# Two-head attention units with one-pass transposes, and modulation products on the matrix engine

## The reference, cut to what matters

```python
def first_block(x, c, ctx, c_ctx, w_ada, b_ada, ...):
    xc = ctx
    s_lat = jax.nn.silu(c)
    s_ctx = jax.nn.silu(c_ctx)
    for l in range(DEPTH):                                   # DEPTH = 2
        mod = (s_lat @ w_ada[l] + b_ada[l])[:, None, :]      # 1024 -> 6 * 1024
        sh1, sc1, g1, sh2, sc2, g2 = jnp.split(mod, 6, axis=-1)
        mod_c = s_ctx @ w_ada[l] + b_ada[l]
        ...
        h = modulate(rmsnorm(x, norm1_g[l]), sh1, sc1)
        hc = modulate(rmsnorm(xc, norm1_g[l]), csh1, csc1)
        p = h @ w_in[l]                # glu 1024, q k v 3 * 512, gates 2048
        ...
        y_conv = conv_branch(...)      # 31 taps over 512 channels, layernorm
        y_attn = merge_heads(neighbourhood_attention(q, k, v, k_c, v_c, na_rpb[l])) @ w_na_out[l]
        x = x + g1 * gated_merge(p[..., QKV_END:], y_conv, y_attn, w_out[l])
        x = x + g2 * conv_ffn(modulate(rmsnorm(x, norm2_g[l]), sh2, sc2), ...)
        if not last:                   # the same for the context, context_attention
            ...                        # over its own 256 keys
```

## Time and profile before

| | us |
|---|---|
| median of 3 runs | 2594.62 |
| lowest and highest | 2591.86, 2596.06 |
| the profiled execution | 2591.45 |
| its span in the profile | 2589.8 |
| mean granted clock of PE, of its full speed | 0.955 |

### The profile page before, as it was taken

The page is one execution under the profiler, slowest core; times in us unless marked ns, Lnnn a source line. Parts: engine busy times, 40 slices in busy tenths (PEclk is TensorE's granted clock), DMA queues, the critical chain, the costliest instruction groups (busy, mean ns, idle before and its releaser), DMA issues.

```text
span 2589.8 us, 49983 instructions
## 1 busy us (share of the span) xinstructions
PE 2318.4 (90%) x18080; PEld 2250.5 (87%) x18080; DVE 1991.8 (77%) x3466; ACT 1254.1 (48%) x1965; POOL 119.9 (5%) x231
## 2 busy tenths in 40 slices
PE   3778699977978999989999999998899999986998
PEld 3767599966878999977999999996899999976998
DVE  7998887969967876896899577668776677687555
ACT  3335266333455654435565454445544544565543
POOL 0000000000000000000000000001000000000000
PEclk9889799988989999989999999998999999998999
DMA  6544555764456555432587667674587587563654
GB/s 252 195 138 153 189 172 180 245 219 133 152 176 203 179 172 185 165 122 90 196 272 262 186 234 261 202 244 156 187 283 242 174 280 252 166 209 95 199 169 135
DMA packets 148461, 500.19 MB, mean 193 GB/s; under 512 B 16480, under 2 KB 17504, under 8 KB 147040
## 3 DMA queue, kind: packets, MB, share of 16 engines
q1 hardware_dynamic: 113472, 375.06, 42.8%
q0 software_dynamic: 32544, 119.03, 15.3%
q10 hardware_dynamic: 2304, 4.20, 0.6%
HBM read 497.16 MB, written 1.05 MB: 192 GB/s over the span
## 4 chain that ended last, share of the span: by engine, by line
PE 67%; DVE 19%; DMA 5%; ACT 4%; issue 4%; DVEq 0%; SPq 0%; POOL 0%; POOLq 0%; ACTq 0%
PE bank_pair L1415 20%; PE bank_pair L1417 20%; PE bank_pair L1416 20%; DVE w_lo L852 4%; DMA modraw<-in_w_mod 4%; DVE arena L1018 3%; DVE modraw L865 2%; DVE x_res L865 2%; PE bank_pair L1590 1%; PE ps_o L1628 1%; PE ps_t L1422 1%; PE ps_t L1601 1%; DVE arena L977 1%; ACT w_hi L494 1%; DVE h_lo L983 1%
## 5 line engine op out<-in xcount | busy, mean ns | idle before, releaser
L852 DVE TENSOR_TENSOR w_lo<-raw,w_hi 128x1024 fp32r<-128x1024 f32 (+3 forms) x772 | 839.9, 1109 | 290.2 <-ACT w_hi L494 287.9
L1415 PE MATMUL bank_pair<-h_hi,w_hi 128*128 128x256 f32 x3344 | 959.6, 287 | 24.6 <-DVE w_lo L852 24.6
L1416 PE MATMUL bank_pair<-h_lo,w_hi 128*128 128x256 f32 x3344 | 952.6, 285 | 0.0
L1417 PE MATMUL bank_pair<-h_hi,w_lo 128*128 128x256 f32 x3344 | 952.3, 285 | 0.0
L494 ACT ACTIVATE w_hi<-raw 128x1024 fp32r<-128x1024 f32 (+3 forms) x772 | 734.3, 964 | 432.9 <-PE bank_pair L1417 327.9
L1415 PEld LDWEIGHTS bank_pair<-h_hi,w_hi 128*128 128x128 f32 x3344 | 648.4, 194 | 36.2 <-DVE w_lo L852 22.5
L1416 PEld LDWEIGHTS bank_pair<-h_lo,w_hi 128*128 128x128 f32 x3344 | 648.7, 194 | 0.2
L1417 PEld LDWEIGHTS bank_pair<-h_hi,w_lo 128*128 128x128 f32 x3344 | 648.3, 194 | 0.0
L1415 PE MATMUL bank_pair<-e_both,w_hi 128*128 128x256 f32 x1774 | 514.7, 290 | 86.5 <-DVE e_both L1369 28.9
L1416 PE MATMUL bank_pair<-e_both,w_hi 128*128 128x256 f32 x1774 | 510.4, 288 | 0.0
L1417 PE MATMUL bank_pair<-e_both,w_lo 128*128 128x256 f32 x1774 | 509.8, 287 | 0.0
(11 more groups left out here) (208 smaller groups left out, 2252.2 us busy)
## 6 DMA issues: line engine op xcount, KB each, us to landing
modraw<-in_w_mod POOLq DMA_DIRECT2D x224, 512.0 KB, 4.6
raw<-in_w_gu SPq DMA_DIRECT2D x176, 512.0 KB, 4.8
raw<-in_w_up SPq DMA_DIRECT2D x132, 512.0 KB, 4.7
raw<-in_w_gate SPq DMA_DIRECT2D x48, 512.0 KB, 4.6
raw<-in_w_dn SPq DMA_DIRECT2D x64, 384.0 KB, 3.6
raw<-in_w_dn SPq DMA_DIRECT2D x64, 320.0 KB, 2.9
raw<-in_w_down SPq DMA_DIRECT2D x48, 384.0 KB, 3.8
raw<-in_w_down SPq DMA_DIRECT2D x48, 320.0 KB, 3.1
```

The costliest lines, as they stand in the source:

```text
L852: nc.vector.tensor_tensor(w_lo[:, p, at], raw[:, p, HALF * f:HALF * f + w], w_hi[:, p, at].bitcast(F32), ALU.subtract).then_inc(lo_ready, 1)
L1415: nc.tensor.matmul(out, l[0], r[0], start=start, stop=False)
L1416: nc.tensor.matmul(out, l[0], r[1], start=False, stop=False)
L1417: return nc.tensor.matmul(out, l[1], r[0], start=False, stop=stop)
```

## The change

There are two parts. **Modulation:** the 33 first blocks leave DVE. The host packs them transposed, so that a 128x128 piece can be PE's weights, and both vectors lie as the two columns of `ccol` (from the new input `vector_cols`). `pe_mod` makes 16 fp32 products of 2 columns for a block into `ps_mod`, four columns of `ps_t`, and ACT copies them to `modcol` (`mod_copy`), which frees `ps_mod`. PE does a block before its slab. At the start PE does blocks 0 and 1, then the sum of the squares, then 2 to 7. In the context branch the blocks are placed anew: one with every slab of glu, q and k, half a block with one of v, none in the gate stage. The load of x no longer waits for the last block and is issued by POOL behind block 8, and SP issues the first slab's first half ahead of blocks 6 and 7. Blocks from 33 on stay on DVE.

**Attention:** a unit is two heads and one tile of queries. The gate slab of unit h goes with it, not one unit later; its sums use all of the first pair of banks (`ps_gate`), the scores the second (`ps_s`). ACT scales the probabilities, so that the transposes are one-pass (`nc.tensor.transpose`) against the plain identity; ACT also copies the context's scores for x. In the context's own attention the maximum and the exponential read PSUM directly. Scores and values take the two heads in turn, on 64 partitions each.

The core of the diff, added lines above all (what they replace is in the functions printed above), with the indentation cut:

```diff
+CONV_AT = np.cumsum([0] + [CONV_SLAB] * 6 + [8] + [3, 8] * 4 + [8]).tolist() + [CONV_K * CONV_C]
...
         early = l == 0 and x == "ctx"
+        stage("glu", a[f"w_glu{l}"], SLAB, 2, mods=1 + early)
+        stage(qk, a[f"w_q{l}"], SLAB, 1, mods=2 if early else int(l == 0), arg=dict(dst="q", rope=rope, scale=HD ** -0.5, conv=(l, 0, 2)))
+        stage(qk, a[f"w_k{l}"], SLAB, 1, mods=2 * early, arg=dict(dst="k" if rope else "kc", rope=rope, scale=1.0, conv=(l, 2, 4)))
         stage("v", a[f"w_v{l}"], SLAB, 1, mods=int(early), arg=dict(dst="v" if rope else "vc", conv=(l, 4, 6), heads=NA_H))
+        stage("gate", a[f"w_gate{l}"], SLAB, 4, mods=int(l == 0 and not early), arg=dict(l=l, ctx=x == "ctx"))
...
+        ps_mod = ps_t[:, 1, 0:4]
+        ps_gate, ps_s = pb
...
+    load(first, 0, 0)
     for k in (6, 7):
+    sp.wait_ge(mod_mm, 2 * (k - 5))
...
+    def mod_copy(m):
+    act.wait_ge(mod_mm, 2 * m + 2)
+    nc.scalar.activation(modcol[:, :, bass.ds(2 * m, 2)], ps_mod.rearrange("p (c v) -> p v c", c=2), ACT.Copy)\
+        .then_inc(mod_done, 2)
+    def mod_copies(s, b, p):
+    if s.m0 < N_DOUBLE:
+        if s.mods == 2:
+            mod_copy(s.m0 + 2 * b + p)
+        if s.mods == 1 and p == 1:
+            mod_copy(s.m0 + b)
...
+    if i == 0:
+        for m in range(2, N_FIRST):
+            if m == 6:
+                split_hi((first, 0, 0), 0)
+                split_hi((first, 0, 0), 1)
+            mod_copy(m)
...
+            if h >= 1:
+                gate_copy(h - 1)
+            at = (h // 2, h % 2, h // 2 == s.bodies - 1)
+            split_hi(following(s, *at), 1)
+            if not is_ctx:
+                act.wait_ge(att_sum, NA_H * n["n_bias"] + h + 1)
+                wait_up(act, att_t, a0 + h - 1)
+                nc.scalar.activation(att_p[:, h % 2, :, 256:512], ps_s[:, :, 256:512], ACT.Copy)\
+                    .then_inc(att_cc, 1)
             act.wait_ge(att_max, a0 + h + 1)
+            if is_ctx:
+                wait_up(act, att_t, a0 + h - 1)
             for t in range(2):
+                scores = ps_s[:, t, 0:keys] if is_ctx else att_p[:, h % 2, t, :]
+                ins = nc.scalar.activation(att_p[:, h % 2, t, 0:keys], scores, ACT.Exp,
                                            bias=small[:, 4 + h % 2, t:t + 1],
                                            accum_out=small[:, 6 + h % 2, t:t + 1])
             ins.then_inc(att_exp, 1)
+            split_hi(after_next(s, *at), 0)
+            act.wait_ge(att_inv, a0 + h + 1)
+            for t in range(2):
+                ins = nc.scalar.activation(att_p[:, h % 2, t, 0:keys], att_p[:, h % 2, t, 0:keys], ACT.Copy,
+                                           scale=small[:, 6 + h % 2, 2 + t:3 + t])
+            ins.then_inc(att_norm, 1)
+        if h == NA_H:
+            gate_copy(h - 1)
...
             act.wait_ge(att_t, a0 + k + 1)
             wait_up(act, att_o, a0 + k - 1)
             nc.scalar.activation(
                 att_pt[:, k % 2, 0:nk, :].rearrange("p k (t q) -> p t k q", t=2),
                 ps_t[:, :, 0:keys].rearrange("p t (k q) -> p t k q", q=P), ACT.Copy).then_inc(att_tc, 1)
         if h >= 2:
+            c, t = (h - 2) // 2, (h - 2) % 2
+            act.wait_ge(att_o, a0 + h - 1)
+            nc.scalar.activation(e_hi[:, CONV_C + c, P * t:P * (t + 1)], ps_o[:, t, 0:P],
                                  ACT.Copy).then_inc(att_hi, 1)
...
             dve.wait_ge(att_s, a0 + h + 1)
+            if is_ctx:
+                scores = ps_s[:, :, 0:keys]
+            else:
+                wait_up(dve, att_t, a0 + h - 1)
+                dve.wait_ge(bias_in[h % 2], 16 * (NA_H // 2 * n_["n_bias"] + h // 2 + 1))
+                nc.vector.tensor_tensor(att_p[:, h % 2, :, 0:256], ps_s[:, :, 0:256], bias[:, h % 2, :, :],
+                                        ALU.add).then_inc(att_sum, 1)
+                scores = att_p[:, h % 2, :, :]
+            if 1 <= h < LN_AT:
+                conv_piece(l, 2 * h + 5, i)
+            if not is_ctx:
+                dve.wait_ge(att_sum, NA_H * n_["n_bias"] + h + 1)
+                dve.wait_ge(att_cc, NA_H * n_["n_bias"] + h + 1)
+            link(nc.vector.tensor_reduce(small[:, 4 + h % 2, 2:4], scores, AXX, ALU.max))
             nc.vector.tensor_scalar(small[:, 4 + h % 2, 0:2], small[:, 4 + h % 2, 2:4], -1.0, None,
                                     ALU.mult).then_inc(att_max, 1)
         if h < LN_AT:
+            conv_piece(l, 2 * h + 6, i)
         if h < NA_H:
+            at = (h // 2, h % 2, h // 2 == s.bodies - 1)
+            split_lo(following(s, *at), 1)
             dve.wait_ge(att_exp, a0 + h + 1)
+            nc.vector.reciprocal(small[:, 6 + h % 2, 2:4], small[:, 6 + h % 2, 0:2]).then_inc(att_inv, 1)
+            split_lo(after_next(s, *at), 0)
         if h >= 2:
...
+            c, t = (h - 2) // 2, (h - 2) % 2
+            at = slice(P * t, P * (t + 1))
+            dve.wait_ge(att_hi, a0 + h - 1)
+            nc.vector.tensor_tensor(e_lo[:, CONV_C + c, at], ps_o[:, t, 0:P],
+                                    e_hi[:, CONV_C + c, at].bitcast(F32), ALU.subtract).then_inc(att_lo, 1)
...
+        if h < NA_H:
+            mods(s, h // 2, h % 2)
...
+    def pe_mod(m, tile, halves=(0, 1), arrived=None):
+    for c in halves:
+        if arrived is not None:
+            pe.wait_ge(mod_in[c], arrived)
+        if c == 0:
+            wait_up(pe, mod_done, 2 * m)
+        for k in range(DC):
+            ins = nc.tensor.matmul(ps_mod[:, 2 * c:2 * c + 2], tile[:, c, P * k:P * (k + 1)], ccol[:, k, :],
+                                   start=k == 0, stop=k == DC - 1)
+        ins.then_inc(mod_mm, 1)
+    def mods(s, b, p):
+    if s.m0 < N_DOUBLE:
+        if s.mods == 2:
+            m = s.m0 + 2 * b + p
+            pe_mod(m, modraw, (0, 1), 16 * (m - N_FIRST + 1))
+        if s.mods == 1:
+            m = s.m0 + b
+            pe_mod(m, modraw, (p,), 16 * (m - N_FIRST + 1))
+    def first_mods(ms):
+    for m in ms:
+        pe.wait_ge(first_in[m], 16)
+        pe_mod(m, mod_first[m % 6])
...
     def body(b, is_first, last):
         for p in range(2):
+            mods(s, b, p)
             operands_ready(s, b, p, is_first)
...
+        first_mods(range(0, 2))
...
     ins.then_inc(sum_ready, 1)
+    if n["i"] == 0:
+        first_mods(range(2, N_FIRST))
...
         if h < NA_H:
+            wait_up(pe, att_exp if is_ctx else att_max, a0 + h)
+            c, t = h // 2, h % 2
+            for n_k, name in enumerate(("kc",) if is_ctx else ("k", "kc")):
+                for hd in range(2):
+                    r = HD * hd
+                    ins = nc.tensor.matmul(ps_s[:, hd, T * n_k:T * (n_k + 1)],
+                                           dst["q"][r:r + HD, c, t * P:(t + 1) * P],
+                                           dst[name][r:r + HD, c, :], start=True, stop=True)
             ins.then_inc(att_s, 1)
+            if h >= 2:
+                free_banks(s, h // 2, h % 2, False)
+            half(s, h // 2, h % 2, 0, h < 2)
+        if 1 <= h <= NA_H:
+            k = h - 1
+            pe.wait_ge(att_norm, a0 + k + 1)
+            wait_up(pe, att_tc, a0 + k)
+            for hd in range(2):
                 for q in range(nk):
+                    ins = nc.tensor.transpose(ps_t[:, hd, q * P:(q + 1) * P],
+                                              att_p[:, k % 2, hd, q * P:(q + 1) * P], table("ident"))
             ins.then_inc(att_t, 1)
         if h == LN_AT:
                 ins = nc.tensor.matmul(ps_o[:, 1, T:2 * T], ones, ln_y[:, k, :], start=k == 0,
                                        stop=k == CONV_C - 1)
             ins.then_inc(ln_var, 1)
+        if h < NA_H:
+            half(s, h // 2, h % 2, 1, h < 2)
         if h >= 2:
+            c, t = (h - 2) // 2, (h - 2) % 2
+            pe.wait_ge(att_tc, a0 + h - 1)
+            wait_up(pe, att_lo, a0 + h - 3)
             for q in range(nk):
+                for hd in range(2):
+                    at = slice(HD * (2 * c + hd), HD * (2 * c + hd + 1))
+                    v = dst["vc"][:, q, at] if is_ctx else \
+                        (dst["v"][:, q, at] if q < 2 else dst["vc"][:, q - 2, at])
+                    ins = nc.tensor.matmul(ps_o[HD * hd:HD * (hd + 1), t, 0:P], v,
+                                           att_pt[:, t, q, hd * P:(hd + 1) * P],
+                                           start=q == 0, stop=q == nk - 1)
             ins.then_inc(att_o, 1)
...
+    for m in range(N_DOUBLE):
+        w = i["w_ada"][m // N_MOD_A][:, 256 * (m % N_MOD_A):256 * (m % N_MOD_A + 1)]
+        a["w_mod"][m] = w.reshape(DC, P, 2, P).transpose(1, 2, 0, 3).reshape(P, 2 * D)
...
+    a["vector_cols"] = np.ascontiguousarray(np.stack([_rows(i["c"][0]), _rows(i["c_ctx"])], 2))
```

190 lines of the change are left out of this document (58 added, 132 removed).

## The result

In ten runs of each kernel the change takes the time from 2594.44 us (2591.31 to 2598.44) to 2599.84 us (2594.36 to 2603.02), a ratio of 1.0021 with a 95% interval of 1.0011 to 1.0031. It is slower, by 5.4 us, clear of the interval but small, where the forecast was 42 slower (2637). In what follows, *before* and *after* are the kernels before and after the change, and a span is the time from the first to the last instruction of the profiled execution: 2595.4 us in after, 2589.8 before.

A forecast was written before the change was run, and what follows sets the result against it. DVE was taken to bound the context branch, PE x's gate stage. At full clock -7-5-15 = -27 us; the clock's fall adds 69, so +42 on the median 2594.6: 2637, range 2562 to 2656.

The forecast's parts named there:

- Case B: Likeliest (0.50): PE's clock falls in the two-column modulation stream, 69 us on top of -27, so +42; own range 2612 to 2658.
- The start: Before the first slab: seven of nine modulation blocks at half clock, +26; with full clock the first slab at 65, +15.
- The fifteen whole blocks: Modulation blocks run whole between slabs: the clock's fall costs 2.4 us each, slab behind included, +36.
- The seventeen half blocks: Modulation blocks in halves between slabs: the clock seldom falls, 1.7 us each when it does, +7.
- Case A: Rival at 0.26: the clock holds at full because loading weights counts; -27 us in all, 2568.
- Merge, out and norm: Context branch: 8 slabs 46, 8 blocks 28, norm 12, together 86 us for 91.6, -6 at full clock.
- The context's gate: Context's gate stage, no modulation blocks left in it: eight units of 9.0 and a tail of 7, 79 for 90.6, -12.
- The ring: Gate stages: DVE and ACT wait on each other, 12.0 us a unit in x's layer 0, 10.8 layer 1, 9.0 context.
- The stretch of down: Down and norm of x: slabs and products 63.4, 8 blocks 28, norm 10.7; 102 us for 95.6, +6.
- Layer 0 of x, to its merge: x's first layer through gate and layernorm to the merge: 730 for 735.7, -5.
- case C: Rival at 0.08: weight load and product don't overlap, 0.19 us a record, 6.1 a block; +86 on the full-clock sum, 2654.
- case E: Rival at 0.09: DVE and ACT's waits are shorter than summed, PE's unit sets x's gate stages; 2530 or 2598.

## Why the prediction was wrong

**The clock's fall: right as a mechanism, mis-sized as a term.** Case B, the likeliest, had the clock fall in the stream of two-column products; the kernel with 128 columns shows that this is its cause. The term was 69 us, and it is 55 (2599.84 less 2544.9). The spans of the two profiled executions differ by 51.8 us, and 50 of them are found in the term's parts. The start was put at 26 for the 19.5 that the first slabs differ by. The fifteen whole blocks were put at 36 for 31 (15.5 and 15.2). The seventeen half blocks were put at 7, where down has the same 99.20 us with and without the fall: 0.

**The sum with the clock held at full: wrong by 23 us, the larger miss.** Case A was -27, and it measured -50 (2544.9 for 2594.95). In the spans it is -46, and the steps below leave 1 to 2 us of that unplaced.
- Merge, out and norm were put at 86 us and are 77.6. The norm was taken at 12 and ends 6 us behind the last slab, and the first of the eight blocks lies ahead of the first merge slab, in a gap of the gate's tail: both were charged here.
- The context's gate was put at 79 and is 74.1, that block included. The ring there was added up as 9.0 us a unit; the maxima come 7.9 apart in the mean.
- The stretch of down was put at 102 and is 99.2.
- Layer 0 of x, to its merge, was put at -5 and is -10.6. The ring is 11.4 us where I had 12.0, and the first units, with the slab in the hole ahead of the second scores, come 9.75 and 10.09 apart. In layer 1 the -15 is -16.0, with 10.26 for 10.8.
- In merge and out of x, 3.8 us less than before were charged to nothing. DVE waits 9.2 us for the modulation's DMA there, for 13.1 before. The same blocks are made in the same place, so this may be their timing; no run isolates it.
- Three steps went the other way. The start at full clock ends at 69.8, not 65, since the second block too runs below full clock in its first part (5.44 us for 3.8), and PE waits 4.2 us ahead of it for ACT's first copy, which stands behind DVE's chain. Glu to v is 87.7 for 86. Up is 1 us longer, where nothing was forecast.

**What held.** The price of a record, 0.11 us, is in the full-clock blocks of every trace; case C (no overlap of load and product) falls. Values did overlap, 16 records of 128 columns in 1.09 us where 8 of 256 had taken 1.94, and so did scores, 8 records in 1.14 for 1.99, for which no row had spoken: both lie near the lower bound of 0.9. PE's unit came out at 9.1 (11.29 us from scores to scores, less the 2.22 of idle time), near the 8.7 of the working, and the ring through DVE and ACT sets the pace instead of it. The ring is 0.5 to 0.6 us shorter than I added up, but case E, in which PE's unit takes its place, did not come. The first slab came at 89.3 for 91 and the clock in the stages with blocks at 0.81 to 0.83, as B has it; the first slab of x came at 587.9, between the 546 named for A and the 613 named for B.

**What failed in the choice.** The fall of the clock was B's, but the time lies outside B's own range of 2612 to 2658. The sign hung on two terms that nearly cancel, 50 gained and 55 lost, so that it came out right is luck as much as foresight. The size was a sum of some ten small terms, most of which erred to the same side: where a bound was open (the norm, the ring, the half blocks), the value taken was the dear one. The whole range, 2562 to 2656, held the time; the forecast of 42 for a loss of 5 was the error.

**The Trainium skill's rule.** Its sentence that the full clock does not engage for PE-mode transposes ("TensorE: Matmul & The Clock Gate", Part 4) was carried over to the modulation. The stream of two-column products did what it says. For the transposes themselves no run tests it: in x's gate stages of after, 8 records of `nc.tensor.transpose` take 1.06 us, 0.11 us apart, which is the pace of full clock (at half clock records stand 0.21 apart). But they come singly between dense products, for a shorter time than the half blocks of 1.71 us, which did not pull the clock down either. So here transposes run at full clock in such a mix; what a long stream of them would do is not shown.

## What to carry to other kernels

A matrix engine that only loads weights and multiplies two columns can be slowed to half, together with the work behind it; widen the moving operand as far as it costs no time (here to 128 columns, for 55 us less), or cut the run into pieces between dense work. Where two parts of a change are written together, time them apart: a gain of 37 us lay hidden under a loss of 43. An engine that begins earlier and then stands idle may pay for it: 12 us of idle time ahead of the squares' sum cost half of the 6 us gained. When an engine is relieved, write out the ring of waits through the others before its own unit is counted as the bound, and look where the wait goes when one link is cut.

## What the runs showed of the hardware

- The granted clock stayed at 0.50 for 32.21 us in which PE was busy all the time (the kernel with idle products between the blocks). With 2 and 32 columns blocks 4 to 7 of the start run at half clock, with 64 and 128 at full.
- Half blocks of 1.71 us between slab halves of 2.9 us left the clock at 0.98, and at 1.00 between the slabs of down; whole ones of 3.49 us between slabs of 5.8 took its mean to 0.83 and 0.81.
- An fp32 product of 2 columns costs PE the same 0.11 us a record as one of 128, at full clock.
- Scores and values of two heads, which use different halves of the array and stand in turn in the queue, take 1.14 and 1.09 us. One head after the other, the same number of columns took 1.99 and 1.94.
- The profile's clock column gives 1.00 for the first two blocks of after (19.07 to 35.70), though they take 6.99 and 6.96 us with records 0.21 us apart, as at half clock. Ahead of the first fall that the column shows, the spacing of the records tells the clock, and the column does not. With 128 columns these blocks take 5.52 and 5.44 us, with their last records at the pace of full clock.
